# Keys turned by VectorE and DMA instead of by TensorE in a hybrid encoder layer

## Time and profile before

| | us |
|---|---|
| median of 3 runs | 1623.04 |
| lowest and highest | 1622.82, 1623.3 |
| the profiled execution's own time | 1623.35 |
| its span, first to last instruction | 1621.6 |

### The profile page before, as it was taken

One profiled execution on the slowest core, in us unless ns is written; L12 is line 12 of the kernel. 1 busy time (PEld: TensorE's weight loads), 2 busy tenths in 40 slices (PEclk: granted clock), 3 DMA queues, 4 the chain that ended last, 5 costly groups with the idle time before them and its releaser, 6 DMA issues.

```text
span 1621.6 us, 24765 instructions
## 1 busy us (share of the span) xinstructions
PE 1616.1 (100%) x8564; PEld 1390.7 (86%) x8564; DVE 1052.3 (65%) x1257; ACT 869.1 (54%) x1192; POOL 25.6 (2%) x30
## 2 busy tenths in 40 slices
PE   9999999999999999999999999999999999999999
PEld 7888888888888888888888888888888888888887
DVE  6865688655656575564755777777777777544443
ACT  6665676466545554555554655555555555433332
POOL 0000121000000000000000000000000000000000
PEclk9999999999999999999999999999999999999999
DMA  8554455655455556555565555655555655565663
GB/s 341 193 194 146 160 171 192 243 191 163 162 184 196 190 181 198 190 190 192 186 196 183 181 182 182 207 190 183 197 181 182 207 191 186 203 203 193 205 207 115
DMA packets 85281, 309.59 MB, mean 191 GB/s; under 512 B 9832, under 2 KB 10352, under 8 KB 84976
## 3 DMA queue, kind: packets, MB, share of 16 engines
q1 hardware_dynamic: 83952, 303.14, 55.7%
q0 software_dynamic: 1136, 5.78, 1.0%
q10 hardware_dynamic: 144, 0.01, 0.0%
HBM read 306.78 MB, written 2.11 MB: 190 GB/s over the span
## 4 chain that ended last, share of the span: by engine, by line
PE 97%; DMA 1%; DVE 1%; SPq 0%; ACT 0%; issue 0%
PE psG L373 94%; PE psM L373 2%; DMA raw<-w_units 1%; DVE W L1035 1%; PE psM L458 0%; PE psM L611 0%; ACT W L676 0%; PE psM L494 0%; PE psM L492 0%; SPq L355 0%; SPq L334 0%; DVE sq_mem L1263 0%; DVE mem_v L1040 0%; DVE sq_mem L1261 0%; DVE sq_x L1258 0%
## 5 line engine op out<-in xcount | busy, mean ns | idle before, releaser
L1035 DVE TENSOR_TENSOR W<-raw,W 128x1024 fp32r<-128x1024 f32 x566 | 688.0, 1228 | 375.4 <-ACT W L676 373.0
L373 PE MATMUL psG<-X,W 128*128 128x512 f32 (+1 forms) x4864 | 845.3, 336 | 0.0
L373 PEld LDWEIGHTS psG<-X,W 128*128 128x128 f32 x4864 | 740.9, 188 | 101.1
L676 ACT ACTIVATE W<-raw 128x1024 fp32r<-128x1024 f32 x566 | 589.8, 1054 | 390.3 <-PE psG L373 373.7
L373 PE MATMUL psG<-W,hidden 128*128 128x512 f32 x1056 | 239.5, 389 | 0.0
L373 PEld LDWEIGHTS psG<-W,hidden 128*128 128x128 f32 x1056 | 198.1, 188 | 41.1
L373 PE MATMUL psG<-W,X 128*128 128x512 f32 x768 | 178.7, 392 | 0.0
L373 PEld LDWEIGHTS psG<-W,X 128*128 128x128 f32 x768 | 143.4, 188 | 29.5
L684 ACT ACTIVATE low<-psG 128x512 f32<-128x512 f32 x100 | 59.7, 597 | 147.5 <-PE psG L373 147.5
L373 PE MATMUL psG<-Y,W 128*128 x768 | 133.1, 335 | 0.0
L373 PEld LDWEIGHTS psG<-Y,W 128*128 128x128 f32 x768 | 116.9, 188 | 15.9
(11 more groups left out here) (191 smaller groups left out, 553.5 us busy)
## 6 DMA issues: line engine op xcount, KB each, us to landing
raw<-w_units SPq DMA_DIRECT2D x566, 512.0 KB, 3.3
xs<-xT SPq DMA_DIRECT2D x4, 512.0 KB, 9.4
x_tok<-x_rows POOLq DMA_DIRECT2D x1, 2048.0 KB, 12.9
mem_raw<-first_data SPq DMA_DIRECT2D x3, 512.0 KB, 5.1
mem_raw<-memT SPq DMA_DIRECT2D x3, 512.0 KB, 7.7
out<-x_tok POOLq DMA_DIRECT2D x3, 512.0 KB, 3.8
lru_rg<-w_rg POOLq DMA_DIRECT2D x8, 128.0 KB, 4.1
c_all<-c_rows POOLq DMA_DIRECT2D x1, 1024.0 KB, 7.2
```

Of the source, the lines that this page charges most:

```text
L373: return nc.tensor.matmul(*a, skip_group_check=True, **kw)
L676: nc.scalar.activation(slots_of(u)[:, s, :, 0], raw[:, s], ACT.Copy).then_inc(hi_done, 1)
L1035: V.tensor_tensor(slots_of(u)[:, s, :, 1], raw[:, s], f32(slots_of(u)[:, s, :, 0]), ALU.subtract).then_inc(lo_done, 1)
```

## The change

The four key groups (mk 0, mk 1, kq 0, kq 2) are no longer transposed by TensorE. After the norm of a key group, VectorE transposes `normed` in squares of 32 within each quarter of the partitions into `key_blocks` (four bytes an element, one instruction over 128x1024). SP then moves the squares to their place with 16 DMAs of 32 partitions, 8 rows of 128 bytes each, four after each of the loads `last + 9` to `last + 12`, into `key_moved_to`. ScalarE copies from there to `kT`, scaled as before, in its step `last + 12`. The query groups are turned as before and at the same units. SP's loop over the loads is written out up to unit 131. The waits are renumbered: `turned` and `turned_out` count queries, the new `key_turned`, `key_moved` and `key_out` count keys.

```diff
-TURN_UNIT = [3, 3, 1, 1, 2, 1, 1, 1]
+KEYS = [_j for _j, (_name, _w) in enumerate(NORMED) if _name == "mk" or _name == "kq" and _w % 2 == 0]
+QUERIES = [_j for _j in range(len(NORMED)) if _j not in KEYS]
+KEY_OUT = 11
+KEY_MOVES = {GROUPS[NORM_GROUP[_j]][3] + 9 + _a: (_n, _a) for _n, _j in enumerate(KEYS) for _a in range(4)}
...
+            def key_move(n, a):
+                blocks = key_blocks["mem" if n < 2 else "fox"]
+                if a == 0:
+                    sp.wait_ge(key_turned, n + 1)
+                    if n > 0:
+                        sp.wait_ge(key_out, n)
+                dst = key_moved_to.rearrange("p t d n -> p (t d) n")
+                for q in range(4):
+                    sp.dma_start(dst[32 * q:32 * q + 32, :, 32 * a:32 * a + 32], blocks[32 * a:32 * a + 32, :, q]).then_inc(key_moved, 16)
+            for u in range(3 * SLOTS, U0["gate0"] + SLOTS):
+                load(u)
+                if u in KEY_MOVES:
+                    key_move(*KEY_MOVES[u])
...
-                      "turned": [GROUPS[g][3] + 5 + n for g, n in zip(NORM_GROUP, TURN_UNIT)],
+                      "turned": [GROUPS[g][3] + 1 + (KEY_OUT if j in KEYS else 5) for j, g in enumerate(NORM_GROUP)],
...
+                if j in KEYS:
+                    n = KEYS.index(j)
+                    act.wait_ge(key_moved, 256 * (n + 1))
+                    if phase == "kq":
+                        dst = att["fox"]["kT"][:, 4 * (w // 2):4 * (w // 2) + 4].rearrange("p d (t n) -> p d t n", t=2)
+                        ins = nc.scalar.activation(dst, key_moved_to.rearrange("p t d n -> p d t n"), ACT.Copy, scale=gk_s[:, 0:1])
+                    else:
+                        dst = att["mem"]["kT"][:, 4 * w:4 * w + 4].rearrange("p (h d) (t n) -> p h d t n", d=2, t=2)
+                        src = key_moved_to.rearrange("p t (h d) n -> p h d t n", d=2)
+                        for d in range(2):
+                            ins = nc.scalar.activation(dst[:, :, d], src[:, :, d], ACT.Copy, scale=gkm_s[:, d:d + 1])
+                    ins.then_inc(key_out, 1)
+                    return
...
+                if j in KEYS:
+                    n = KEYS.index(j)
+                    if n > 0:
+                        dve.wait_ge(key_moved, 256 * n)
+                    dve.wait_ge(evac_done, g + 1)
+                    V.transpose(key_blocks["mem" if n < 2 else "fox"].rearrange("p e q j -> p (e q j)"),
+                                normed.rearrange("p t c -> p (t c)")).then_inc(key_turned, 1)
...
-            wide_group("mk", 1, m_op, {TURN_UNIT[0]: turn(0)})
+            wide_group("mk", 1, m_op, {})
-            wide_group("mq", 0, x_op, {TURN_UNIT[1]: turn(1)}, ready=x_ready)
+            wide_group("mq", 0, x_op, {}, ready=x_ready)
-            wide_group("kq", 1, x_op, {TURN_UNIT[4]: turn(4, dve=side_count("decay", 0, "dve", "z"))})
-            wide_group("kq", 2, x_op, {TURN_UNIT[5]: turn(5), **attention_hooks("fox", 0)})
+            wide_group("kq", 1, x_op, {})
+            wide_group("kq", 2, x_op, {1: turn(5, dve=side_count("decay", 0, "dve", "z")), **attention_hooks("fox", 0)})
```

More of the change, by code:

```diff
@@ L199, in hybrid_layer_kernel @@
         square = {"mem": sb("mem_square", [P, 2, 2 * UC], 121 * KB), "fox": sb("fox_square", [P, 2, 2 * UC], 109 * KB)}
+        key_blocks = {"mem": sb("mem_key_blocks", [P, 8, 4, 32], 125 * KB), "fox": sb("fox_key_blocks", [P, 8, 4, 32], 104 * KB)}
+        key_moved_to = sb("key_moved_to", [P, 2, 4, P], T0 + 4 * KB + 512)
         lx_pad = sb("lx_pad", [P, 2, 3 + T], M0)
@@ L277, in hybrid_layer_kernel @@
             sem("head_squares"), sem("head_root"), sem("head_inverse"), sem("turned"), sem("turned_out")
+        key_turned, key_moved, key_out = sem("key_turned"), sem("key_moved"), sem("key_out")
         ss_done, rstd_done = sem("ss_done"), sem("rstd_done")
@@ L357, in _ @@
             sp.dma_start(ff_raw[:], w_ff).then_inc(ff_in, 16)
-            with sp.Fori(3, U_ALL // SLOTS) as i:
+            def key_move(n, a):
[11 more added lines that the diff above has]
+                    key_move(*KEY_MOVES[u])
+            with sp.Fori(U0["gate0"] // SLOTS + 1, U_ALL // SLOTS) as i:
                 for s in range(SLOTS):
@@ L447, in hook @@
                 def hook():
-                    if j == 0:
+                    n = QUERIES.index(j)
+                    if n == 0:
                         pe.wait_ge(const_in, 48)
@@ L451, in hook @@
                     else:
-                        pe.wait_ge(turned_out, j)
+                        pe.wait_ge(turned_out, n)
                     side_waits(**banks_free)
@@ L463, in attention_hooks @@
                 A = att[kind]
-                last_turn = {"mem": [2, 3], "fox": [5, 6, 7, 7]}[kind][m]
-                own_turn = {"mem": [2, 3], "fox": [5, 5, 7, 7]}[kind][m]
+                turned_before = {"mem": [1, 2], "fox": [3, 3, 4, 4]}[kind][m]
                 def scores():
-                    pe.wait_ge(turned_out, own_turn + 1)
+                    pe.wait_ge(key_out, turned_before)
+                    pe.wait_ge(turned_out, turned_before)
                     side_waits(dve=side_count(kind, m, "dve", None), act=side_count(kind, m, "act", None))
@@ L484, in transposes @@
                 def transposes():
-                    pe.wait_ge(turned_out, last_turn + 1)
+                    pe.wait_ge(turned_out, turned_before)
                     side_waits(dve=side_count(kind, m, "dve", "weights1"))
@@ L568, in _ @@
             wide_group("mk", 0, m_op, {0: mem_sums, 4: x_sums})
-            wide_group("mk", 1, m_op, {TURN_UNIT[0]: turn(0)})
+            wide_group("mk", 1, m_op, {})
             x_ready = lambda n: pe.wait_ge(xX_lo, n // 2 + 1)
-            wide_group("mq", 0, x_op, {TURN_UNIT[1]: turn(1)}, ready=x_ready)
-            wide_group("mq", 1, x_op, {TURN_UNIT[2]: turn(2), **attention_hooks("mem", 0)})
-            plain("lru", None, {TURN_UNIT[3]: turn(3, act=side_count("mem", 0, "act", "weights_copied")), **attention_hooks("mem", 1)})
+            wide_group("mq", 0, x_op, {}, ready=x_ready)
+            wide_group("mq", 1, x_op, {1: turn(2), **attention_hooks("mem", 0)})
+            plain("lru", None, {1: turn(3, act=side_count("mem", 0, "act", "weights_copied")), **attention_hooks("mem", 1)})
             with pe.Fori(1, 4) as i:
@@ L578, in _ @@
             wide_group("kq", 0, x_op, {})
-            wide_group("kq", 1, x_op, {TURN_UNIT[4]: turn(4, dve=side_count("decay", 0, "dve", "z"))})
-            wide_group("kq", 2, x_op, {TURN_UNIT[5]: turn(5), **attention_hooks("fox", 0)})
-            wide_group("kq", 3, x_op, {TURN_UNIT[6]: turn(6, act=side_count("fox", 0, "act", "weights_copied")), **attention_hooks("fox", 1)})
-            plain("gate0", None, {TURN_UNIT[7]: turn(7, act=side_count("fox", 1, "act", "weights_copied")), **attention_hooks("fox", 2)})
+            wide_group("kq", 1, x_op, {})
+            wide_group("kq", 2, x_op, {1: turn(5, dve=side_count("decay", 0, "dve", "z")), **attention_hooks("fox", 0)})
+            wide_group("kq", 3, x_op, attention_hooks("fox", 1))
+            plain("gate0", None, {1: turn(7, act=side_count("fox", 1, "act", "weights_copied")), **attention_hooks("fox", 2)})
             plain("gate0", 1, attention_hooks("fox", 3))
@@ L721, in turned_copied @@
                 phase, w = NORMED[j]
-                act.wait_ge(turned, j + 1)
+                if j in KEYS:
[11 more added lines that the diff above has]
+                    return
+                act.wait_ge(turned, QUERIES.index(j) + 1)
                 src = psM[:, 0:2, :].rearrange("p h (d t) -> p h d t", d=2)
                 if phase == "kq":
-                    dst = att["fox"]["qT" if w % 2 else "kT"][:, 4 * (w // 2):4 * (w // 2) + 4].rearrange("p (h d) t -> p h d t", d=2)
-                    ins = nc.scalar.activation(dst, src, ACT.Copy, scale=p1("g_q", 0) if w % 2 else gk_s[:, 0:1])
+                    dst = att["fox"]["qT"][:, 4 * (w // 2):4 * (w // 2) + 4].rearrange("p (h d) t -> p h d t", d=2)
+                    ins = nc.scalar.activation(dst, src, ACT.Copy, scale=p1("g_q", 0))
                 else:
-                    dst = att["mem"]["qT" if phase == "mq" else "kT"][:, 4 * w:4 * w + 4].rearrange("p (h d) t -> p h d t", d=2)
+                    dst = att["mem"]["qT"][:, 4 * w:4 * w + 4].rearrange("p (h d) t -> p h d t", d=2)
                     for d in range(2):
-                        ins = nc.scalar.activation(dst[:, :, d], src[:, :, d], ACT.Copy,
-                                                   scale=p1("g_qm", d) if phase == "mq" else gkm_s[:, d:d + 1])
+                        ins = nc.scalar.activation(dst[:, :, d], src[:, :, d], ACT.Copy, scale=p1("g_qm", d))
                 ins.then_inc(turned_out, 1)
@@ L952, in quarter @@
                                              ).then_inc(merged_hi, 1)
+            act.wait_ge(key_out, len(KEYS))
             quarter(0, first=True)
@@ L1069, in norm @@
```

(6 more changed lines are left out.)

## The result

| | before | after |
|---|---|---|
| median us | 1623.04 | 1626.63 (9 runs) |
| lowest and highest | 1622.58, 1624.92 (9 runs beside it) | 1624.35, 1629.32 |
| profiled execution, its span | 1623.35, 1621.6 | 1624.35, 1622.5 |
| ratio after / before, 95% interval | | 1.0022 (1.0013 to 1.0031) |

A forecast was written before the change was run, and what follows sets the result against it. TensorE was taken as the bound, with 97% of the chain. From the profiled 1623.35, -3.5 for turns and +0.6 for a stall gave 1620.45, or 1620.1 as median (1623.04 - 2.9); range 1619.5 to 1623.5.

The forecast's parts named there:

- Removed turns, -3.5: TensorE, after units 27, 35, 106 and 121: four key turns of 0.87 us leave the chain, 3.5 us off.
- Transpose, 1.22 + 0.03; stall of 0.59 at unit 29: VectorE's transpose delays everything behind it by 1.25 us; split 29 then comes late and TensorE stalls 0.59 us.
- I take 0.44 a move, nearest to the small transfers of SP: SP's queue: issuing one move takes 0.44 us, from rows giving 0.33 to 0.44, and 1.32 once.
- the 1.32 row: One 1.32 us issue of 128 pieces in the earlier trace, read as standing behind a full queue; evidence for slow moves.
- 87.6 + 8p + 3.3: First key group: landing time of load 35 when each move costs SP p us.
- Cover of 0.80 at unit 36: Second key group: split 36 ends at 105.24, unit 35 at 106.38, leaving 0.80 us before TensorE would wait.
- changes nothing that the chain passes: SP's loop unrolled to unit 131: takes register work off an issue, no effect on the time.
- In the other groups the splits are 5 units' work ahead, nothing shows: Moves of the key groups after the first: ScalarE's splits lead by 5 units' work, so they cost nothing.
- Rival C: Moves at 1.32 us hold up loads 33 to 35; 6.6 us stall at unit 36, 1626.7 us; chance 0.18.
- break-even of 1.0 us a move: Unit 36: at 1.0 us a move late load 35 cancels the gain; between about 0.6 and 1.0 it eats it.

The follow-up runs named there:

- second ten executions of the changed kernel: The changed kernel run again with no edit, for a second profile; 1626.46 us, ratio 1.0017 to the kernel before.
- spread kernel: Changed kernel with each group's sixteen moves on SP as 3, 3, 3, 3, 2, 2 behind six loads, scaled copy two steps later; 1626.18 us, ratio 1.0018.
- GpSimd kernel: Changed kernel with GpSimd issuing the moves: 1620.81 us (again 1620.79); with key transposes four steps later also, 1620.45; with `x_tok` load behind fox moves too, 1619.61.
- moves and transposes: Kernel before plus unrolled SP loop, sixteen moves a group on SP and VectorE's four transposes into unread buffers, TensorE's turns kept; 1624.72 us, ratio 1.0010.

## Why the prediction was wrong

- *Removed turns, -3.5*: right, 3.57 by the ledger.
- *Transpose, 1.22 + 0.03; stall of 0.59 at unit 29*: right, 1.246 and 0.62. The count unit by unit was worth its length.
- *"I take 0.44 a move, nearest to the small transfers of SP"*: wrong, 0.65. Of my two sorts of rows the larger was no better guide: the 1.32 row was read as a full queue, and its sum would be 6.6 us at unit 36. The formula for load 35, 87.6 + 8p + 3.3, gives 96.1 with p = 0.65, and it landed at 96.45 (a load behind moves takes 0.60 to issue and 4.07 to land).
- *Cover of 0.80 at unit 36*: it was gone, and 0.99 of wait came. Split 36 ended at 106.23, not at 105.24: load 35 came at 96.45, and with it the norm was late. And TensorE wanted it earlier: 0.26 from unit 0 (chance) and 0.55 from unit 16, which I had put down as "changes nothing that the chain passes". In its trace SP's load 12 leaves at 25.25 instead of 25.80; the time itself doesn't show it.
- *"In the other groups the splits are 5 units' work ahead, nothing shows"*: this is the step that made the kernel slower. It counts the lead of splits, but in these steps ScalarE also makes the squares for the next query group, and TensorE's query turn waits for that norm, not for a split. The cover there was 0.64 us (122.84 to 123.48), and the turn after 113 had 0.11 (349.69 to 349.80). I checked the turns that were removed and none of those that stayed. Both ends of that chain were moved by the change: load 40's gate by the transpose and late load 35, and load 43 by the three lots of moves ahead of it.
- *Rival C* (moves hold up loads, slower) named the right mechanism at the wrong place. Its break-even of 1.0 us a move was for unit 36 alone; at the turn after 41 about 0.65 is too much already, once the transposes are there. That its time, 1626.7, is 0.1 from the measured one is luck: it came from 6.6 us at unit 36, where 0.99 were measured, and from nothing elsewhere.
- *What the ledger of the profiled execution leaves*: it is 0.9 above before's, the medians are 3.6 apart. Of the second ten executions of the changed kernel the five with a mean granted clock of 1.000 took 1624.59 to 1626.09, the five with 0.999 took 1626.83 to 1627.0; of the first nine, three with 1.000 took 1624.35 to 1626.03 and six with less 1626.61 to 1629.32. Of 106 executions of the kernel before, beside the experiments, one had 0.999. The half clock that the spread kernel's windows show after a long wait before a turn would fit: eight of that kernel's eleven executions had 0.999 or less, the profiled one among them. No profile of the changed kernel caught it, and a mean of 0.999 alone doesn't prove it (a GpSimd kernel's execution of 1620.08 us has 0.999 too, with 1.00 in its windows up to 1616.5 us), so for the changed kernel this part is argued, not shown. What makes the waits at unit 104 was settled only for the GpSimd kernels, by moving `x_tok`; for the changed kernel it is open, as is how much of them the moves on SP bring.

## What to carry to other kernels

When DMAs are put into the queue that feeds the bound engine, sum the issue times of everything between one load's gate and the next load that somebody waits for, and follow that load to every consumer: the side work behind a split as well as the split. Before you give a removed wait as gain, read the cover of the waits that stay. If another engine has an idle queue, small transfers belong there: here that, with the transpose out of VectorE's full stretch and a large load behind the moves, turned +3.6 us into -3.2.

## What the runs showed of the hardware

- **An issue on SP costs by the DMA.** 32 KB from SBUF to SBUF: 0.61 us in 256 pieces, 0.59 in 32, where a 512 KB load takes 0.33, or 0.60 right behind such moves. The data took 1.9 to 3.9 us to land with 128-byte pieces (median 2.5) and 1.8 to 3.5 with 1 KB (median 2.4). The Trainium skill (DMA: Bandwidth & Descriptors, Why small descriptors are slow (HBM only)) says that transfers within SBUF don't suffer from small pieces; these landings agree.
- **Long issues lie beside instruction fetches.** An issue of SP now and then takes 0.9 to 2.2 us: 31 times in the 14 traces, and beside each of them a transfer of an instruction queue is on its way, in 30 cases one of 16 KB (at 336.16 us in the trace of moves and transposes, where the issue takes 1.55 us, one of 8 KB). In the second run of the changed kernel, three moves took 3.54 us instead of 1.9, and the DMA view of 337.3 to 339.6 shows one (packets, MB, share):

```profile
336.80 3.54 SPq L376 DMA_DIRECT2D key_moved_to<-fox_key_blocks  x3
```

```profile
q8 instruction: 1, 0.02, 5.7%
```

The 1.32 us of the earlier trace rows has one beside it too (one such transfer in the DMA view of 23.0 to 24.5 us). In the changed kernel's trace the same DMA took 0.44 us, and the long issue (1.52) is another one, at 21.78, where the transfer now lies. So the 1.32 gave no ground to blame a full queue. That the fetch is the cause was not tried.
- **TensorE's clock falls after a long wait.** In the spread kernel's trace TensorE stood still for 2.55 us before the turn; the granted clock was 1.00 until 125.4, then 0.56 and 0.83 as means of the next two windows, a stretch at the lower of its two levels (1.2 GHz). Unit 42 took 4.39 us more than before; after took 2.38 more with 2.15 of standing still, so 4.39 - 2.55 - 0.23 = 1.6 us is, by estimate, the clock. The changed kernel's 2.15 us, and 2.36 in its second trace, brought no fall: the windows from 118 to 134 us of both have 1.00 throughout. The page can't tell this: a 9 in its clock row means 90% or more, and the spread kernel's page too has 9 in all 40 slices. The Trainium skill (TensorE: Matmul & The Clock Gate, Part 1: The HAM clock gate) has half rate as the state of an idle TensorE; here it agrees in one trace.
